# The two streams of the double norms one behind the other, and the short-range heads first in the second block's attention

## The reference

```python
def first_block(x, c, ctx, ...):
    hx, hc = x, ctx
    for i in range(2):
        ax = _modulate(hx, norm1_g[i], sx1, cx1)       # rms_norm(h) * (1 + scale) + shift
        ac = _modulate(hc, norm1_g[i], sc1, cc1)
        yx, yc = mixer(ax, ac, ...)                    # projections, rotary, attention, w_out
        hx = hx + gx1 * yx
        hx = hx + gx2 * _mlp(_modulate(hx, norm2_g[i], sx2, cx2), mlp_w1[i], mlp_w2[i])
        if i == 0:
            hc = hc + gc1 * yc
            hc = hc + gc2 * _mlp(_modulate(hc, norm2_g[i], sc2, cc2), mlp_w1[i], mlp_w2[i])
    return _rms_norm(hx, final_g)

def second_block(x, c, ...):
    for l in range(2):
        h = x * (1 + scale) + shift
        (p_cq, p_ckv, p_kr, p_qb, p_kb, p_vb, p_qc, p_kc, p_vc, p_qi, p_ki, p_wi, p_gate) = split(h @ w_in[l])
        cq, ckv = rms_norm(p_cq, q_norm_g[l]), rms_norm(p_ckv, kv_norm_g[l])
        qa, ka, va = cq @ w_uq[l], ckv @ w_uk[l], ckv @ w_uv[l]
        o_a = mla_attention(...)        # 6 heads, causal, with a rotary part
        o_b = dilated_attention(...)    # 6 heads of short-range windows, from p_qb, p_kb, p_vb
        o_c = sparse_attention(...)     # 4 heads, only the 64 best keys of an index score
        y = concat(o_a, o_b, o_c) * silu(p_gate)
        x = layer_norm(ALPHA * x + (1 + gate) * (y @ w_out[l]), ln_g[l], ln_b[l])
```

## Time and profile before

| | us |
|---|---|
| median of 3 runs | 1389.36 (1388.78 to 1389.87) |
| the profiled execution | 1389.1 |
| its span in the profile | 1387.3 |
| PE busy | 1327.9 (96% of the span) |
| DVE busy | 991.2 (71%) |
| ACT busy | 670.5 (48%) |
| mean granted TensorE clock | 0.974 |

### The profile page before, as it was taken

One profiled execution on the slowest core, in us unless ns is written; L12 is line 12 of the kernel. 1 busy time (PEld: TensorE's weight loads), 2 busy tenths in 40 slices (PEclk: granted clock), 3 DMA queues, 4 the chain that ended last, 5 costly groups with the idle time before them and its releaser, 6 DMA issues. The chain is left out here.

```text
span 1387.3 us, 24593 instructions
## 1 busy us (share of the span) xinstructions
PE 1327.9 (96%) x9158; PEld 1161.7 (84%) x9158; DVE 991.2 (71%) x1722; ACT 670.5 (48%) x1348; POOL 192.8 (14%) x274
## 2 busy tenths in 40 slices
PE   7999998999999999989999899999999998899987
PEld 6786776888888888878896899999899978899967
DVE  6798786899887877976339565565665985765974
ACT  4437743531624316343238564466455565465663
POOL 0101212000000000212006600000220016020034
PEclk9999998999999999989999999999999999899989
DMA  8782133467985858825220345765374533355601
GB/s 319 262 247 91 53 116 122 152 212 227 306 300 206 303 201 294 282 70 149 86 92 1 113 143 161 206 184 179 125 265 154 181 108 116 127 178 166 197 32 47
DMA packets 67657, 234.85 MB, mean 169 GB/s; under 512 B 7280, under 2 KB 12400, under 8 KB 67312
## 3 DMA queue, kind: packets, MB, share of 16 engines
q1 hardware_dynamic: 67568, 233.67, 51.8%
HBM read 232.59 MB, written 1.05 MB: 168 GB/s over the span
## 5 line engine op out<-in xcount | busy, mean ns | idle before, releaser
L849 DVE TENSOR_TENSOR wlo<-raw,whi 128x1024 fp32r<-128x1024 f32 x284 | 349.9, 1233 | 172.1 <-ACT whi L551 165.0
L551 ACT ACTIVATE whi<-raw 128x1024 fp32r<-128x1024 f32 x284 | 299.4, 1055 | 246.6 <-PE ps L1475 244.0
L1473 PE MATMUL ps<-Hh,whi 128*128 128x512 f32 (+1 forms) x848 | 297.7, 351 | 10.2 <-DVE Hl L985 8.3
L1474 PE MATMUL ps<-Hl,whi 128*128 128x512 f32 (+1 forms) x848 | 294.5, 347 | 0.0
L1475 PE MATMUL ps<-Hh,wlo 128*128 128x512 f32 (+1 forms) x848 | 294.2, 347 | 0.0
L1473 PEld LDWEIGHTS ps<-Hh,whi 128*128 128x128 f32 x848 | 162.4, 191 | 35.9 <-issue 11.8
L1473 PE MATMUL ps<-Gh,whi 128*128 128x256 f32 x624 | 178.1, 285 | 3.8 <-DVE Gl L985 3.8
L1475 PEld LDWEIGHTS ps<-Hh,wlo 128*128 128x128 f32 x848 | 162.3, 191 | 21.5
L1474 PEld LDWEIGHTS ps<-Hl,whi 128*128 128x128 f32 x848 | 162.4, 191 | 20.6
L1474 PE MATMUL ps<-Gl,whi 128*128 128x256 f32 x624 | 176.9, 284 | 0.0
L1475 PE MATMUL ps<-Gh,wlo 128*128 128x256 f32 x624 | 176.8, 283 | 0.0
(11 more groups left out here) (232 smaller groups left out, 2043.0 us busy)
## 6 DMA issues: line engine op xcount, KB each, us to landing
raw<-wall SPq DMA_DIRECT2D x284, 512.0 KB, 4.3
aring<-aall SPq DMA_DIRECT2D x144, 512.0 KB, 4.7
AL<-ali SPq DMA_DIRECT2D x14, 192.0 KB, 5.3
X<-xin SPq DMA_DIRECT2D x2, 1024.0 KB, 6.4
BI<-rpb SPq DMA_DIRECT2D x4, 512.0 KB, 10.0
out<-X SPq DMA_DIRECT2D x4, 256.0 KB, 2.3
cst<-const SPq DMA_DIRECT2D x1, 960.0 KB, 8.5
par<-prm SPq DMA_DIRECT2D x1, 134.5 KB, 2.1
```

The costliest lines, as they stand in the source:

```text
L551: act.activation(whi[:, slot, :], raw[:, slot, :], ACT.Copy).then_inc(sem("w_hi"), 1)
L849: dve.tensor_tensor(wlo[:, slot, :], raw[:, slot, :], whi[:, slot, :].bitcast(F32), ALU.subtract)\
L1473: pe.matmul(o, a[0], b[0], start=first, stop=False)
L1474: pe.matmul(o, a[0], b[1], start=False, stop=False)
```

## The change

Two parts.

**Streams apart.** For `l0b` and `l1a` the last three units before the norm (5 to 7 of eight, from `HALVED` on) are multiplied in two passes of 256 columns: first the x half of all three, then the c half of all three (PE `halves`). DVE adds the x halves, and x is squared, summed and given its root while PE works on c; its sums and its spread stand on PE behind the first and second c half. The next matrix starts with three units on x alone (`first_stream`), with the sums and the spread of c inside it; after `l0b` the c half of those three follows (`second_stream`). After `l1a` the first three units are queries, which need x only; the order of the 16 units of that projection is changed (`L1_ORDER`), so that five query units come before the first key unit, and the c half of the norm is modulated by DVE and ACT between the preparations of units (`L1_SECOND`). PE's wait for the last `ada_ready` now stands ahead of the first x half in the MLP, and DVE does the products of step 13 and `ada_sums` ahead of its first half addition. The quarters 0 and 3 are written out where a loop ran before. One product of the output projection is moved a step earlier (`ADA_L0`).

**Short range first.** In both layers of the second block the three short-range jobs come first. The scores of the first two of them are made on PE behind the second unit of `p_uq`, their maxima on DVE behind the rotary of that unit, their exponentials on ACT behind the evacuations of the third and fourth unit. `p_uq`, `uk` and `uv` go to banks 4 to 7 for that. The mask of the sparse heads is made inside the attention's pipeline, ahead of the fourth job's maxima (`select`). The output projection takes its row tiles in the order of the jobs.

```diff
-ADA_L0 = (0, 0, 0, 0, 1, 1, 1, 2, 1, 2, 1, 0, 5, 0, 0, 1, 0, 1, 0, 0)
+ADA_L0 = (0, 0, 0, 0, 1, 1, 1, 2, 1, 2, 1, 0, 5, 0, 0, 1, 1, 0, 0, 0)
...
+HALVED = 5
+OUT_BANKS = ((1, 2, 4), (5, 0, 3))
+MLP_BANKS = ((0, 1, 4), (5, 2, 1))
+L1_ORDER = (0, 1, 2, 3, 4, 8, 9, 10, 5, 11, 6, 12, 7, 13, 14, 15)
...
+            def last_halves(u, n):
+                square(n, HALVED - 1)
+                for k in range(HALVED, KT):
+                    square_x(n, k)
+                for k in range(HALVED, KT - 1):
+                    ahead(u + k - HALVED + 1)
+                    square_c(n, k)
+                hi_x(n, 0)
+                hi_x(n, 1)
+                square_c(n, KT - 1)
+                for k in range(2, KT):
+                    hi_x(n, k)
...
                             act.activation(M[:, j % 2, 0:T], Y[:, j % 2, 0:T], ACT.Square).then_inc(sem("hid_a"), 1)
                             act.wait_ge(sem("hid_a"), 8 * it + (h0 + j + 1))
                             act.activation(HIDh[:, j, 0:T], M[:, j % 2, 0:T], ACT.Copy).then_inc(sem("hid_h"), 1)
+                        elif last and last.pair is not None and j == 8 + HALVED:
+                            last_halves(u0 + 16 * it + j, last)
+                            return
...
+                for k in L1_SECOND[i]:
+                    hi_c(norms["l1a"], k)
...
                 for i in range(5):
                     ahead(u0 + 37 + i)
                     evac(p_uq[l], i)
+                    if i in (2, 3):
+                        exps(J_B2[l][0] + i - 2)
                 ahead(u0 + 42)
...
+                attend(*J_B2[l], begun=2)
...
+            def last_halves(u, n, add, name, early):
+                def half(k, v):
+                    if v:
+                        dve.wait_ge(sem("w_used"), u + k - HALVED + 1)
+                    else:
+                        dve.wait_ge(sem("half_used"), 3 * n.pair + k - HALVED + 1)
+                    add(k, v).then_inc(sem(name if v else "added_x"), 1)
+                half(HALVED, 0)
+                early()
+                half(HALVED + 1, 0)
+                half(HALVED + 2, 0)
+                half(HALVED, 1)
+                variance_of(n, 0)
+                ahead(u + 1)
+                half(HALVED + 1, 1)
+                dve.wait_ge(sem("spread_x"), n.pair + 1)
+                scaled(n, 0, 0)
+                scaled(n, 1, 0)
+                ahead(u + 2)
+                low(n, 0, 0)
+                low(n, 1, 0)
+                half(HALVED + 2, 1)
+                scaled(n, 2, 0)
+                for k in range(2, KT):
+                    if k + 1 < KT:
+                        scaled(n, k + 1, 0)
+                    low(n, k, 0)
+                    if k == 3:
+                        variance_of(n, 1)
...
+                    if select is not None and s == j0 + 3:
+                        dve.tensor_scalar(IX[:, :], IX[:, :], -2.0e38, NEG, ALU.is_gt, ALU.mult).then_inc(sem("sel_done"), 1)
+                        dve.wait_ge(sem("sel_done"), select + 1)
+                        dve.tensor_tensor(AL[:, 6:10, :], AL[:, 6:10, :], IX[:, None, :].to_broadcast([P, 4, 384]), ALU.add)\
+                           .then_inc(sem("sb_done"), 1)
+                        dve.wait_ge(sem("sb_done"), select + 1)
                     if j0 + begun <= s < j1:
...
+                        if last and j == 8 + HALVED:
+                            ada_dots(it, j)
+                            ada_sums(it)
+                            last_halves(16 * it + u0 + j, n, gated_half(s, 40, MLP_BANKS), "mlp_added", early)
+                            return
                         if ada and j == 0:
...
+            add_out(U_L0_OUT, 0, gated(0, 16, 512), 12, HALVED)
+            ahead(U_L0_OUT + HALVED)
+            last_halves(U_L0_OUT + HALVED, norms["l0b"], gated_half(0, 16, OUT_BANKS), "out_added", rows_l0b)
+            second(norms["l0b"], 0, KT)
+            mlp(U_L0_MLP, 0, 512, 0, ada=True, n=norms["l1a"], early=rows_l1a)
+            for i in range(L1_FM):
+                ahead(U_L1 + i)
+                for k in L1_SECOND[i][:1]:
+                    second(norms["l1a"], k, L1_SECOND[i][-1] + 1)
+                for k in L1_ROPES[i]:
+                    rope(p_l1, k)
+            rope(p_l1, L1_FM - 1)
             for v in range(8):
                 if v >= 6:
...
+                steps(p_uq[l], 0, 3)
+                maxima(J_B2[l][0])
+                steps(p_uq[l], 3, 4)
+                maxima(J_B2[l][0] + 1)
+                steps(p_uq[l], 4, 5)
                 ahead(u0 + 42)
                 ahead(u0 + 43)
-                dve.wait_ge(sem("ali_landed"), 16 * (10 + 4 * l))
-                dve.wait_ge(sem("sel_done"), l + 1)
-                dve.tensor_tensor(AL[:, 6:10, :], AL[:, 6:10, :], SEL[:, None, :].to_broadcast([P, 4, 384]), ALU.add)\
-                   .then_inc(sem("sb_done"), 1)
-                dve.wait_ge(sem("sb_done"), l + 1)
...
+            def halves(n, units, banks, x, free):
+                for v in range(2):
+                    for i, u in enumerate(units):
+                        if v == 0:
+                            pe.wait_ge(sem("w_lo"), u + 1)
+                        free(i, v)
+                        for k in range(KT):
+                            ins = mm3(ps[:, banks[v][i], 0:N], wtile(u % SLOTS, P * k, P),
+                                      (x[0](k)[:, N * v:N * v + N], x[1](k)[:, N * v:N * v + N]), k == 0, k == KT - 1)
+                        ins.then_inc(sem("w_used" if v else "half_used"), 1)
+                        if v == 1 and i == 0:
+                            sums_of(n, 0)
+                        if v == 1 and i == 1:
+                            spread_of(n, 0)
...
+            def first_stream(n, units, banks, x):
+                for u in units:
+                    pe.wait_ge(sem("w_lo"), u + 1)
+                for k in range(KT):
+                    pe.wait_ge(sem("low_x"), 8 * n.pair + k + 1)
+                    for u, bank in zip(units, banks):
+                        ins = mm3(ps[:, bank, 0:N], wtile(u % SLOTS, P * k, P), (x[0](k)[:, 0:N], x[1](k)[:, 0:N]),
+                                  k == 0, k == KT - 1)
+                        if k == KT - 1 and n.pair == 1:
+                            ins.then_inc(sem("w_used"), 1)
+                    if k == 1:
+                        sums_of(n, 1)
+                    if k == 4:
+                        spread_of(n, 1)
...
+                    if tail is not None:
+                        def free(i, v):
+                            if v == 0 and i == 0:
+                                pe.wait_ge(sem("ada_ready"), ADA_GROUPS + QUARTERS)
+                            elif v == 1 and i == 1:
+                                pe.wait_ge(sem("mlp_added"), 8 * it + (1 + h0 + HALVED))
+                            elif v == 1 and i == 2:
+                                pe.wait_ge(sem("added_x"), 3 * tail.pair + 2)
+                        halves(tail, range(u0 + 16 * it + 8 + HALVED, u0 + 16 * it + 16),
+                               MLP_BANKS, (lambda k: HIDh[:, k, :], lambda k: HIDl[:, k, :]),
+                               free)
...
+            project_out(U_L0_OUT, 0, 512, Hx, ("o_lo", [HL[3 * k + 2] for k in range(KT)]),
+                        norm=norms["l0b"])
...
+            pe.wait_ge(sem("mlp_added"), 8 * (QUARTERS - 1) + 1 + HALVED + 2)
+            pe.wait_ge(sem("added_x"), 4)
+            first_stream(norms["l1a"], range(U_L1, U_L1 + TOGETHER), [(p_l1.o0 + i) % 4 for i in range(TOGETHER)], Hx)
+            project(p_l1, TOGETHER, L1_ORDER.index(8), Hx)
+            pe.wait_ge(sem("nlo"), norms["l1a"].h0 + KT)
+            project(p_l1, L1_ORDER.index(8), L1_FM, Hx)
...
+                project(p_uq[l], 0, 2, Cx, kts=6)
+                pe.wait_ge(sem("proj_out"), p_uq[l].o0)
+                scores(J_B2[l][0])
+                scores(J_B2[l][0] + 1)
+                project(p_uq[l], 2, 5, Cx, kts=6)
...
                 pe.wait_ge(sem("rope_out"), p_uq[l].r0 + 2)
-                attend(*J_B2[l])
-                project_out(u0 + 44, 16 + 8 * l, 256, Gx, ("o_lo", [HL[J_B2[l][0] + k] for k in range(KT)]))
+                attend(*J_B2[l], begun=2, values_out=V_UV[l] + 2)
```

More of the change, by code:

```diff
@@ L221, in __init__ @@
                 self.direct = direct
+                self.pair = None
         def adacol(s, v, t):
@@ L1173, in gated, with mlp, quarter @@
                 return add
-            def mlp(u0, h0, T, s, ada=False):
-                def quarter(it):
+            def mlp(u0, h0, T, s, ada=False, n=None, early=None):
+                def quarter(it, last=False):
                     def lo(j):
@@ L1567, in spread, with sums_of, part @@
                 ins.then_inc(sem("spread"), 1)
+            def sums_of(n, v):
+                if v == 0:
+                    pe.wait_ge(sem("modded"), n.t0)
+                    pe.wait_ge(sem("sqx_used"), 2 * (n.pair + 1))
+                else:
```

(35 more changed lines are left out.)

232 lines of the change are left out of this document (160 added, 72 removed).

## The result

| | before | changed |
|---|---|---|
| median of 10 runs, us | 1389.44 (1387.23 to 1390.75) | 1393.43 (1391.04 to 1397.08) |
| ratio | | 1.0024, 95% interval 1.0015 to 1.0034 |
| span of the profiled execution | 1387.3 | 1391.4 |
| PE busy | 1327.9 | 1322.6 |
| mean granted TensorE clock | 0.974 | 0.976 |

A forecast was written before the change was run, and what follows sets the result against it. PE, busy 1327.9 of 1387.3 us, was taken as the bound, so only its pauses and low clock could shorten. Terms -7.5 + 7.7 + 2.4 + 1.5 = +4.1 on 1389.1 gave 1393.2, median 1393.5; range 1383 to 1399.5.

The forecast's parts named there:

- l0b: Norm l0b, output projection's unit 4 to first 72 MLP matmuls: pause and low clock go, 44.1 to 36.6 us, -7.5.
- The wait at unit 13: At l1a, PE idles 9.35 us ahead of unit 13 until DVE's products and sums are done, starting at 589.1.
- long met: At l1a before the change, PE's wait for the last ada_ready behind unit 15 was taken as already satisfied.
- The low clock behind it: At l1a, behind PE's wait ahead of unit 13: half clock after the pause costs 2.5 us.
- the extra 0.85: At l1a, two new c stream pauses may drop the clock again: 0 to 1.7 us, taken as 0.85.
- The c stream's pauses: At l1a, PE waits for c's modulation and preparation: +1.4 us before the fourth unit, +2.95 before the first key unit.
- Second block: Attention of both layers: moved maxima and exponentials delay uv, PE idle 5.4 us; +2.4 in one layer, +1.5 in the other.
- The edits put at nothing: Product a step earlier in the output projection, quarters written out, row tile order, two-way bank choice: zero effect.
- The second block gains after all: Rival: the fill works at the attention's start, about 5.5 us a layer, total -10.8, 1378.6 us; chance 0.11.
- The wait at unit 13 is harmless: Rival: DVE's sums done by 579.8, so l1a gives -5; total -8.6, 1380.8 us; chance 0.08.
- not as it says at l0b: Rival: PE still waits for x there, low clock after it; -7.5 becomes -2, 1399 us; chance 0.03.
- Clock lost at every new pause: Rival: l1a +10, second block +8, l0b -6, total +12, 1401 us; chance 0.1 for 1398 and above.

The follow-up runs named there:

- the last experiment, mask_early: Changed kernel with PE's wait and ACT's exponentials both moved later, plus the sparse heads' mask made ahead of the second job's maxima: 1372.57 us, ratio 0.9865.
- exps_late: Changed kernel with ACT's first second-block exponentials behind the fourth query unit's evacuation and the second ones behind that of uv: 1380.36 us, ratio 0.9925.
- the one with both moves: Changed kernel with PE's last ada_ready wait only ahead of the sums of x and the second block's exponentials moved later on ACT: 1368.15 us, ratio 0.9844.
- wait_late: Changed kernel with PE's wait for the last ada_ready moved from ahead of unit 13 to ahead of the sums of x: 1383.36 us, ratio 0.9954.
- norms_wait_late: Changed kernel with both norms' streams apart and PE's ada_ready wait moved to the sums of x, second block's attention as before: 1380.15 us, ratio 0.9932.
- l1a_only: Kernel before with only norm l1a's streams apart, PE's wait ahead of unit 13; l0b and attention as before: 1399.18 us, ratio 1.0069.

## Why the prediction was right, point by point

- **l0b, -7.5 forecast, -7.4 measured.** PE never waited for x; pauses add up to 0.4 us, and both the 8.4 us and the low clock went. The x half of unit 7, called the closest, didn't wait.
- **The wait at unit 13, 9.35 forecast, 8.80 measured.** DVE's chain ran as listed, step by step. Of the 0.55 us, 0.45 are its first step: DVE began the addition 0.17 us behind the unit's end (574.10 to 574.27), where the forecast had 0.62 (579.75 to 580.37). One premise was wrong and did no harm: before, the last `ada_ready` was not "long met" behind unit 15. By the profile PE stood 1.27 us for it there too, ahead of the sums (the row is below), and those 1.27 us lie in the 617.2 of before to which the forecast counted.
- **The low clock behind it, 2.5 forecast, 2.9 measured;** the extra 0.85 for the two short pauses of the c stream didn't come: the window 612 to 680 has clock 1.00. As a mean of 0 and 1.7 it was fair all the same. The same two pauses stand in seven traces, and in three of them 1.7 us were lost behind them (last section).
- **The c stream's pauses, 1.4 and 2.95 forecast, 1.58 and 2.58 measured.** `l1a` in all +7.7 against +6.9, the 0.85 being most of it.
- **Second block, +2.4 and +1.5 forecast, +1.8 and +1.4 measured.** Pause ahead of `uv` 5.4 against 5.01; third maxima 25.5 us after the first query unit against 25.0 (1133.07 less 1108.04); from there to the last 17.1 against 17.0. But inside that last number a term was mis-sized: 2.5 us were put down for the mask, and the last experiment shows 0.7 for it. The other 1.8 may belong to the pace of the mla jobs, which now stand behind the short-range ones; no run separates that.
- **The sum: +4.1 forecast, +2.8 measured in the changed stages.** The whole came to +4.1 only because 1.4 us arose where nothing was changed: +1.8 at the start, +1.4 between the blocks, -1.8 between the two layers. The hit to 0.1 us is luck to that extent; the forecast of the terms is good to 0.8 us each. The edits put at nothing gave nothing that the ledger shows: the quarters written out lie in the stretch from 253 to 574 us, which is 0.0.
- **The rivals.** "The second block gains after all" was right about the size (5.5 a layer; exps_late gains 4.8 and 5.8 over before) and wrong about the point from which it decides. I had put it at the first maxima on DVE, to be done by 1113.5 (8 us after the first query unit). In exps_late they start as late as in the changed kernel (9.5 us after it, in both), and the gain is there. It decides on ACT, where an instruction that waits for those maxima stood ahead of an evacuation and two preparations. "The wait at unit 13 is harmless" and "not as it says at l0b" are refuted by the rows above. "Clock lost at every new pause" holds in this trace for the pauses of 5 and 9 us and not for those of 1.6 and 2.6; three other traces have it for those too.

The row of before for the wait that was called long met (PE's sums at `l1a`):

```profile
597.34 1.05 PE L1525 MATMUL ps<-cst,RS 128*128 128x2 f32 x8 [1.27 <-DVE ada L938]
```

## What to carry to other kernels

When work is moved forward to fill a pause, look at what is queued behind each of its instructions on its engine: here the exponentials were early enough, but they waited for DVE with an evacuation behind them that PE needed, and two calls moved on ACT were worth 13 us. A wait that guards a bank belongs ahead of the first instruction that writes the bank, not at the start of the phase; moved there, it was hidden by four half units of matmul. The pauses of 5.0 and 8.8 us cost their own length and another 1.5 to 3 us of low clock behind them. Breaking a pause up is no sure way out of that: two pauses of 1.6 and 2.6 us cost nothing more in four traces and 1.7 us in three.

## What the runs showed of the hardware

The same short pauses can leave the granted clock alone or not. The c stream of `l1a` stops PE for 1.5 to 1.6 us and, one unit later, for 2.6 us in seven traces. These are the 12 us from the first of the two on, in the changed kernel and in the one with both moves:

```profile
618.60:630.60 12.00, 9.34 (x51) 7.94 (x52) 8.25 (x19) 5.32 (x10) 2.01 (x3) 1.00 0.36 123
```

```profile
608.50:620.50 12.00, 9.38 (x44) 7.90 (x45) 8.23 (x19) 5.34 (x10) 2.03 (x3) 0.86 0.39 120
```

`wait_late`, `exps_late` and `mask_early` have 1.00 there too, `norms_wait_late` and `l1a_only` 0.86 as well. 0.14 of 12 us is 1.7 us. In the kernel before, pauses of 1.49 and 2.91 us at `l0b` stood ahead of a group at 0.87; the prediction's "pauses of 4 us and up" holds only for their sum. No run says what decides between the two.

The granted clock also moves time between stages that are the same in both programs. Behind the first layer of the second block, where nothing was changed and the engines do the same work, the window of the changed kernel (1180 to 1204) and that of before (1176 to 1200) read:

```profile
1180.00:1204.00 24.00, 18.29 (x126) 17.53 (x125) 14.51 (x32) 8.13 (x16) 4.73 (x6) 0.79 0.21 67
```

```profile
1176.00:1200.00 24.00, 18.35 (x113) 17.34 (x112) 13.20 (x31) 6.56 (x13) 4.33 (x5) 0.72 0.19 62
```

0.79 against 0.72 over 24 us is 1.7 us, the 1.8 of the ledger. All ten traces have one of these two values there: 0.79 in the five kernels that have both norms and the second block changed, in whatever variant, 0.72 in the five others, the one with only the second block changed among them. With one trace each, no run here says whether the combination decides it or where the stretch happens to fall. A term of under 2 us that is read from a difference of two whole spans can be this alone. Read from the stage's own two ends it is safer but not sure: the attention in the old order took 48.9 to 50.5 us from one trace to the other. The start of the program differs too: ACT's fifth `whi` begins at 52.10 us before, at 53.86 in the changed kernel and at 53.06 to 54.99 in the eight others, where none of the parts of the change has begun.
